# New orders of the steps on TensorE, ScalarE and VectorE in a two-block, two-layer kernel

## What is computed

```python
# block 1, for each of 2 layers
h = _rms(x, norm_g[l]); proj = h @ w_in[l]                     # 17 parts
y_a = _gla(gq, gk, gv, ga, ...) * silu(gz)                     # branch a: gated linear attention
y_b = _dsa(bq, bk, bv, iq, ik, iw, ...) * silu(bz)             # branch b: top-k attention
y_c = _diff(cq, ck, cv, ...) * silu(cz)                        # branch c: differential attention
merged = g[:, :, 0]*(y_a @ w_br[l,0]) + g[:, :, 1]*(y_b @ w_br[l,1]) + g[:, :, 2]*(y_c @ w_br[l,2])
x = x + merged @ w_out[l]
# inside _dsa: which keys a query may see
score = einsum('bqhs,bqh->bqs', relu(dots), iwb);  top_val, top_idx = lax.top_k(score, 128)
# inside _gla: the decay of a token
log_a = log_sigmoid(a_lr @ wa2 + ba) / GLA_TAU
# block 2, for each of 2 layers
mod = silu(c) @ w_mod[l] + b_mod[l]                            # six rows of 1024
h = rms_norm(x, norm1) * (1 + scale1) + shift1; proj = h @ w_in
y_pool = pool_mixer(u, ...); y_nsa = nsa_mixer(q, k, v, gates, ...)  # compressed + selected + window
x = x + gate1 * (concat([y_pool, y_nsa]) @ w_out)
h2 = rms_norm(x, norm2) * (1 + scale2) + shift2
x = x + gate2 * (square(relu(h2 @ w_ff1)) @ w_ff2)             # width 4096
```

## Time and profile before

| | us |
|---|---|
| three runs | 2622.38, 2625.09, 2625.36 |
| median | 2625.09 |
| profiled execution: span | 2625.7 |
| PE busy | 2471.4 (94%) |
| DVE busy | 1365.9 (52%) |
| POOL busy | 1280.2 (49%) |
| ACT busy | 954.5 (36%) |
| mean granted TensorE clock | 0.972 of full |

### The profile page before, as it was taken

How to read it: one execution, slowest core, us unless ns; L and a number is a source line. 1 busy time by engine, 2 the same in 40 slices (tenths; PEclk the granted TensorE clock), 3 DMA queues, 4 the chain that set the end, 5 groups by cost and what they waited for, 6 DMA issues and landing times.

```text
span 2625.7 us, 36622 instructions
## 1 busy us (share of the span) xinstructions
PE 2471.4 (94%) x12303; PEld 1982.3 (75%) x12303; DVE 1365.9 (52%) x2835; ACT 954.5 (36%) x1691; POOL 1280.2 (49%) x2900
## 2 busy tenths in 40 slices
PE   7989999999998999999998898999998889899999
PEld 6676878678867687867887657888888656788887
DVE  5596343654459624365366445554467754522325
ACT  4433243432443234343244553322224354332221
POOL 4453736356545273635644104676765301466563
PEclk9999999999999899999999899999999999999999
DMA  4231514135423151413532002454534101233332
GB/s 160 87 97 50 176 49 144 49 105 184 134 65 97 52 173 57 137 49 113 180 97 61 25 1 65 153 167 146 165 120 109 53 17 30 68 97 96 97 96 81
DMA packets 132193, 256.18 MB, mean 98 GB/s; under 512 B 21914, under 2 KB 28588, under 8 KB 132012
## 3 DMA queue, kind: packets, MB, share of 16 engines
q1 hardware_dynamic: 132012, 253.83, 30.9%
HBM read 249.60 MB, written 4.19 MB: 97 GB/s over the span
## 4 chain that ended last, share of the span: by engine, by line
PE 80%; DVE 14%; ACT 3%; issue 2%; POOL 0%; DMA 0%; DVEq 0%; SPq 0%; ACTq 0%
PE ps L826 66%; PE ps L780 4%; DVE arena L1778 2%; DVE top L1776 2%; PE ps L1077 2%; PE ps L973 1%; PE ps L1126 1%; PE ps L888 1%; PE ps L953 1%; DVE maskb L1783 1%; PE ps L948 1%; PE ps L1064 1%; DVE ps L1714 1%; DVE yarena L1966 1%; ACT arena L1439 1%
## 5 line engine op out<-in xcount | busy, mean ns | idle before, releaser
L757 POOL TENSOR_TENSOR wl<-raw,wh 128x128 fp32r<-128x128 f32 (+2 forms) x2896 | 1280.0, 482 | 1318.8 <-ACT wh L1147 1317.6
L826 PE MATMUL ps<-wh,hTh 128*128 128x512 f32 (+3 forms) x1600 | 637.6, 398 | 3.1 <-POOL wl L757 1.9
L826 PE MATMUL ps<-wl,hTh 128*128 128x512 f32 (+3 forms) x1600 | 618.4, 387 | 0.0
L826 PE MATMUL ps<-wh,hTl 128*128 128x512 f32 (+3 forms) x1600 | 618.2, 386 | 0.0
L1147 ACT ACTIVATE wh<-raw 128x1024 fp32r<-128x1024 f32 (+2 forms) x362 | 378.2, 1049 | 523.1 <-PE ps L826 287.5
L826 PEld LDWEIGHTS ps<-wh,hTh 128*128 128x128 f32 x1600 | 306.2, 191 | 77.6 <-issue 16.7
L826 PEld LDWEIGHTS ps<-wh,hTl 128*128 128x128 f32 x1600 | 305.5, 191 | 58.9
L826 PEld LDWEIGHTS ps<-wl,hTh 128*128 128x128 f32 x1600 | 306.2, 191 | 51.1
L826 PE MATMUL ps<-hTh,wh 128*128 128x512 f32 (+2 forms) x704 | 259.0, 368 | 3.9 <-DVE hTl L1718 2.4
L826 PE MATMUL ps<-hTh,wl 128*128 128x512 f32 (+2 forms) x704 | 257.7, 366 | 0.0
L826 PE MATMUL ps<-hTl,wh 128*128 128x512 f32 (+2 forms) x704 | 257.7, 366 | 0.0
(11 more groups left out here) (274 smaller groups left out, 3199.3 us busy)
## 6 DMA issues: line engine op xcount, KB each, us to landing
raw<-in_w_in_dram SPq DMA_DIRECT2D x160, 512.0 KB, 3.6
raw<-in_w_ff_dram SPq DMA_DIRECT2D x128, 512.0 KB, 3.7
modw<-in_w_mod_dram SPq DMA_DIRECT2D x96, 512.0 KB, 4.7
raw<-in_w_br_dram SPq DMA_DIRECT2D x24, 512.0 KB, 3.7
raw<-in_w_out_dram SPq DMA_DIRECT2D x24, 512.0 KB, 3.6
xm<-in_x_dram SPq DMA_DIRECT2D x8, 512.0 KB, 4.1
raw<-in_w_out_dram SPq DMA_DIRECT2D x16, 256.0 KB, 3.7
raw<-in_w_in_dram SPq DMA_DIRECT2D x8, 408.0 KB, 3.2
```

What stands on the lines that cost most here:

```text
L757: last = pool.tensor_tensor(low[part], whole[part], high[part], ALU.subtract)
L826: last = pe.matmul(*args, start=(q == 0 and c == 0 and n_pass == 0), stop=(q == u["quarters"] - 1 and c == u["chunks"] - 1 and n_pass == 2))
```

## The change

Only tables and the code that reads them are changed: no operation is added, taken away or given another size. `FIRST` and `SECOND` list the same steps in another order. `MOVED` has a third table, for PE, and the two for ACT and DVE are longer, several hundred pairs in all. Evacuations and `mod` steps can now be named in it, for one layer or both. PE's moves are applied first, and ACT's and DVE's sequences start from PE's; SP's loads, the weight halves and the scratch slots go by PE's sequence. The norm heads keep their places. Of the diff, cut to a line or two of each table:

```diff
 FIRST = """
-index.2.0 index.2.1 bk.1.0/ index.2.2 index.2.3 bk.1.0 index.2.4 index.2.5 bk.1.1/ index.2.6 index.2.7 bk.1.1
...
+index.2.1 topk.1.0 index.2.2 index.2.3 bk.0.3 bk.1.0/ index.2.4 bk.1.0 index.2.5 bk.1.1/ index.2.6 index.2.7
...
+topk.3.7 topk.3.8 decay1.2 gv.1.3 gz.0.0 topk.3.9 gz.0.1 decay1.3 gz.0.2 gz.0.3 decay3.0 gz.1.0 decay3.1
...
-MOVED = {"act": """prob_turn.b.0.0>logit_exp.b.0.2 pair_exp.2.0.0>pool_band.1 pair_exp.1.1.2>pool_band.1 logit_exp.c.3.3>gate11.1.1
...
+MOVED = {"pe": """evac.bq.1>bq.1.0 q_turn.b.1>bq.1.2 evac.iq.0>iq.1.3 evac.small.0>index.0.4
...
+                  evac.fd60.0>fd61.0.1 evac.fd60.1>evac.fd60.0 evac.fd61.1>evac.fd61.0 fd71.0.1>evac.fd71.0
...
+                  mod.6.0>bz.1.3 mod.5.0>y_tok.a.2 mod.4.0>bz.0.1 mod.3.0>index.0.4 mod.2.0>iq.1.3
...
+                  prob.c.1.3>logit_max.c.2.0 prob.c.2.0>prob.c.1.3 evac.br10.0>logit_max.c.2.1
```

More of the change, by code:

```diff
@@ L106 @@
[L106 to L109, removed]
-bz.0.3 y_turn.a.1 gla_out.3 y_tok.a.3 y_turn.a.2 bz.1.0 bz.1.1/ bz.1.1 bz.1.2 y_turn.a.3 bz.1.3 gate00.0.0
@@ new lines @@
+pair_value.0.0 cmp_logits.1 pair_value.0.1 rstd.eq.1 pair_logits.1.1.0 pair_turn.1.0.0 pair_prob.1.0.0
+pool_band.0 pair_prob.1.0.2 pair_max.1.1.2 pair_prob.1.1.0 cmp_turn2.1 pair_logits.1.1.2 pair_prob.1.1.2
+o_split.0 pair_logits.2.0.0 pair_turn.1.0.2 pair_exp.1.0.0 pair_max.2.0.0 pair_exp.1.0.2 pool_band.1
+pair_exp.1.1.0 cmp_prob.2 cmp_logits.2 pair_value.1.0 pair_prob.2.0.0 pair_prob.2.0.1 pair_max.2.0.1
+pair_max.2.0.2 pair_max.2.0.3 pair_turn.1.1.0 pair_exp.1.1.2 pool.0 pair_logits.2.0.1 pair_turn.1.1.2 cmp_prob.3
@@ new lines @@
+pool.1 pair_logits.2.0.2 pair_turn.2.0.0 pair_exp.2.0.0 pair_value.1.1 cmp_turn2.2 pair_exp.2.0.1
+pair_prob.2.0.2 pair_prob.2.0.3 pair_exp.2.0.2 pair_exp.2.0.3 pair_logits.2.0.3 pair_turn.2.0.1 pair_exp.2.1.0
+pair_logits.2.1.0 pair_turn.2.0.2 pair_max.2.1.0 o_split.1 pool_band.2 pair_turn.2.0.3 pair_max.2.1.1
+pair_exp.2.1.1 pair_logits.2.1.1 pair_exp.2.1.2 pair_turn.2.1.0 pair_logits.2.1.2 pair_prob.2.1.0 pair_max.2.1.2
+pair_prob.2.1.1 cmp_logits.3 cmp_in.1 pair_exp.2.1.3 pair_logits.2.1.3 pair_logits.3.0.0 pair_exp.3.0.0
@@ new lines @@
+pair_turn.2.1.1 pair_prob.2.1.2 pool.2 pair_max.2.1.3 pair_value.2.0 pair_turn.2.1.2 pair_logits.3.0.1
+pair_max.3.0.0 pair_turn.2.1.3 pair_prob.2.1.3 pair_logits.3.0.2 pair_exp.3.0.1 cmp_turn2.3 pool_band.3
+pair_turn.3.0.0 pair_prob.3.0.0 pair_prob.3.0.1 pair_prob.3.0.2 pair_max.3.0.1 pair_prob.3.0.3 pair_value.2.1
+pair_logits.3.0.3 pair_exp.3.0.2 pair_turn.3.0.1 pair_exp.3.0.3 pair_max.3.0.2 pair_logits.3.1.0 pair_exp.3.1.0
+pool.3 pair_turn.3.0.2 pair_logits.3.1.1 pair_turn.3.0.3 pair_logits.3.1.2 pair_prob.3.1.0 pair_exp.3.1.1
@@ L193, in steps @@
             out.append((kind, named[rest[0]], *rest[1:]))
+        elif kind in ("stats", "scale", "turn"):
+            out.append((kind, (rest[0], l), *rest[1:]))
+        elif kind == "mod":
+            out.append((kind, rest[0]))
+        elif kind in ("columns", "constants"):
+            out.append((kind,))
         else:
@@ L335, in orders @@
 def orders(line, units):
-    own = {"pe": line}
-    for engine, moved in MOVED.items():
-        own[engine] = seq = list(line)
+    own = {}
+    for engine in ("pe", "act", "dve"):
+        own[engine] = seq = list(own["pe"] if own else line)
         for l in sorted({u["l"] for u in units}):
             named = {u["name"]: i for i, u in enumerate(units) if u["l"] == l}
-            for pair in moved.split():
+            for pair in MOVED[engine].split():
                 step, place = (steps(word, l, named)[0] for word in pair.split(">"))
-                seq.remove(step)
-                seq.insert(seq.index(place) + 1, step)
+                if step[0] not in ("mod", "columns", "constants") or pair.split(">")[0].endswith(f".{l}"):
+                    seq.remove(step)
+                    seq.insert(seq.index(place) + 1, step)
@@ L395, in build @@
     own = orders(line, units)
+    line = own["pe"]
     start = []
```

325 lines of the change are left out of this document (234 added, 91 removed).

## The result

| | us |
|---|---|
| changed kernel, four runs | 2527.9 to 2533.96, median 2530.03 |
| kernel before, four runs | 2622.22 to 2625.36, median 2623.74 |
| ratio | 0.9638 (0.9622 to 0.9654, 95%) |
| profiled execution, span | 2528.0 (before 2625.7) |

The account below looks back on a forecast made before the run. PE was taken as the bound, busy 2471.4 of 2625.7 us. From 2625: -26 for block 1's waits, -26 for block 2's, -12 for the clock, +9 for new waits, giving 2570 us, range 2540 to 2624.

Parts of the forecast that it names:

- decay1.3: Block 1's decay step: PE's 7.6 us wait for DVE's top-k chain goes, -6.9 a layer, bounds -3.3 and -7.6.
- The GLA wait: Block 1's GLA output: the first wait, 3.6 us, grows by about 1.5; all its waits together +0.6.
- The transposes behind L1457: Block 2's second and third tiles: waits of 2.8 and 2.5 us for ACT's copy shrink by 2.4 and 1.9.
- prob_turn.c.1.3: Block 1's differential attention: a 3.7 us wait behind DVE's evacuation of br10.0 falls to about 1.4, -2.3.
- I count half: Block 1's shorter waits, 1.3 us and less, sum to about 7; half taken as gain, -3.7.
- I take 3 back: Block 2's listed gains of -15.9 a layer, cut by 3 for new waits between coupled steps, to -12.9.
- a fifth to a quarter: Clock term: share regained of 51 us lost to lowered clock in three attention stages, -12, bounds 0 and -30.
- +9: New waits elsewhere: a microsecond or so in nine rearranged places, bounds 0 and +25.
- index and key: Block 1's index and key waits: 1.6 us, of which -0.8 goes, bounds 0 and -1.6.
- rival A: Whole kernel: all waits go as listed, 58 us, and 20 of clock: 2547 us, chance 0.17.
- Rival D: Whole kernel slower: mod products stall ahead of evacuations while POOL runs, up to 2660 us, chance 0.13.
- The mask that I had expected to meet POOL idle: Block 1's top-k: the 7.79 us mask, moved earlier, meets POOL idle and the chain ends 7.3 us sooner.

Follow-up runs that it names:

- decay_alone: Kernel before, with PE's decay1.3 alone moved behind two sweep steps, DVE's top-k as before: 2630.52 us, ratio 1.0016.
- br10_alone: Kernel before, with only DVE's evacuation of br10.0 moved behind a later probability step: 2620.82 us, ratio 0.9988.
- decay_shift: Kernel before, with decay1.3, the decay3 steps and the four state steps of PE moved to their changed places: 2613.71 us, ratio 0.9965.
- block1_new: New orders on all three engines up to block 1's last sweeps, the old orders behind: 2586.79 us, ratio 0.9883 to the kernel before.
- attn2_new: New orders in the two attention stages of block 2 alone, old orders elsewhere: 2546.64 us, ratio 0.9741 to the kernel before.
- filler: Kernel before, with 52 transposes that nobody reads put on PE ahead of decay1.3: 2617.47 us, ratio 0.9972.
- undo_pair: Changed kernel, with PE's pair_turn.1.0.2 put back directly behind cmp_turn2.1 in both layers: 2532.99 us, ratio 0.9635 to the kernel before.

## Why the forecast was wrong

**What held.** PE bounds the kernel, and waits and clock are all that an order can give: 72.6 of 154.3 us of idle and 25.1 of busy time went, nothing else. `decay1.3` was forecast at -6.9 a layer and gave -7.6 and -7.4. That it came so near is partly luck: the release was forecast at 192.3 and came at 194.1, PE was forecast at 192.5 and came at 195.6, and the two errors, 1.8 and 3.1 us, go the same way and nearly cancel. The GLA wait was forecast to stay and stayed (3.7, forecast 4 to 5 and growing; it was 3.6). The transposes behind L1457: forecast -2.4 and -1.9, and 2.8 and 1.8 went. `prob_turn.c.1.3`: forecast -2.3, measured -3.7. Of my signs, PE's idle was to be about 110 and is 81.7, and one sign of a wrong forecast came: a new wait of over 2 us in the feed-forward (3.24).

**The step that failed** is the one by which I took the sum apart: "I count half", "I take 3 back", "a fifth to a quarter", and "+9" for new waits. Each is a discount on what the rows listed, and none has a row. What the runs showed in their place:

| term | forecast | measured |
|---|---|---|
| waits of block 1, both layers | -26 | -38 |
| waits of block 2's attention | -26 | -38 |
| clock | -12 | -25 |
| new waits, feed-forward included | +9 | +5 |

The measured rows are from the two tables of stages above: length less PE's busy time for the waits, the change of the whole busy time for the clock, and the idle of the feed-forward for the last; new waits inside a stage with new orders are in its net. In block 1 the short waits were the largest miss: of the differential attention's stage, 6.7 us with the 3.7 of `prob_turn.c.1.3`, 5.4 and 6.6 us went, and all 2.3 of index and key. In block 2 no wait over 0.8 is left in the attention behind the norm head, where there had been seven of over 1.3. That is rival A, which I gave 0.17 and 2547, and which itself stopped at 20 us of clock and 58 of waits.

**Why the discount was tempting and wrong.** I feared that a wait taken away comes back at the next place. It does: `decay_alone` and `br10_alone` gained nothing, the wait moved on to a step behind it. But this is so of a single move. `decay_shift` moved all that hangs on one chain at once and won 4 of 7.6 us by that on PE's side alone (DVE's top-k, which the change also starts earlier, untouched), and `block1_new` with `attn2_new` show no loss between the stages. That the many other waits went for the same reason is argued from this one case and not shown wait by wait. The test that I should have made is in the orders and in the trace: for each step behind the freed one, whether it too has work put ahead of it. For the decay step I had looked at `decay1.3` only; the change also moves `decay3` and the state steps, and without that, by `decay_alone`, PE's part of my -6.9 would have been near 0.

**What the decay wait was.** I priced 7.6 us as the length of top-k, and the stall of the mask as something beside it. The unheld masks of `attn2_new` and `filler` show that the stall is nearly all of the wait. The new order of top-k puts the mask where DVE has gaps behind it, so that the wait goes and stays away; against a layer in which the mask isn't held, this term is 0.3 us.

**The clock.** I held that a fifth to a quarter of 51 us would come back; 25 did, and 24 of this net are from the attention of block 2 (block 1 gave 5, the feed-forward took 4). Its stages held 42 of the 51 by my own figures. `attn2_new` won 29 us of busy time in them. Behind the decay wait the clock was 0.60 over six microseconds before and 1.00 in `attn2_new`, which had no such wait. But in `undo_pair` one wait of 2.0 among few others cost nothing that can be seen at the clock. That it takes many waits close together, as between the second and the fourth token tile of block 2 before, is what the traces suggest and no run isolates. There the same steps in the same order took 68.7 us in layer 0 and 60.4 in layer 1 of the kernel before (clock 0.78 and 0.92), 64.2 and 67.3 in `filler` (and as much in `br10_alone`, which has no filler), 61.7 and 60.5 in `decay_shift`. The kernel before, then the changed one:

```profile
1461.60:1530.30 68.70, 58.41 (x318) 38.02 (x318) 31.36 (x67) 30.83 (x80) 0.00 (x0) 0.78 0.00 1
2111.40:2171.80 60.40, 49.50 (x318) 31.53 (x317) 31.26 (x67) 30.83 (x80) 0.00 (x0) 0.92 0.00 1
```

```profile
1406.80:1452.40 45.60, 44.08 (x312) 28.28 (x310) 32.07 (x70) 33.75 (x81) 11.82 (x26) 0.96 0.00 1
2028.70:2075.80 47.10, 45.57 (x312) 28.98 (x310) 32.00 (x70) 33.74 (x81) 11.77 (x26) 0.93 0.00 1
```

The stretch that answers to it in the changed kernel takes 45.6 and 47.1 (312 matmuls where it was 318). So part of the loss comes and goes in one and the same order. Which of the waits bring the clock down stays open: the waits of that stretch weren't filled, since all eight banks are in use there.

**Rival D** had its mechanism seen (a `mod` step and POOL's run ahead of an evacuation, 3.24 us at `fu1.1.0` and 1.7 for the slow step behind it, 4.56 us where it is 2.88), once where it needed seven. It cost 5 us of the 8 that the stage became longer. The product ended at 1580.67, 1.08 us behind the end of POOL's run of 13.94 us (1579.59), so it got to work only when that run was over. The page "SBUF — State Buffer" of the Trainium skill, section "SBUF: two separate sides", has the lock held "for the whole instruction", by which the product would wait for one subtraction; this trace too disagrees, since POOL's run is 32 of them. The mask that I had expected to meet POOL idle took 3.13 us instead of 7.79, also within a run: the stall was shortened and not gone, and the term didn't need it, since 6.47 us of idle stand behind it.

## What to carry to other kernels

When many steps are moved together, price each wait by asking whether everything that hangs on the same chain has work put in front of it; if so count all of the wait, and if not, count little of it, since it moves on. A flat discount for coupling fits neither case. Look along the chain for an instruction far over its median, as the mask of 7.79 us beside 0.66: a wait that hangs on it comes and goes by itself, and a time can be compared only when the trace says which case it was. Where the trace shows a stage with a lowered clock and dense short waits, give the clock a term of its own and let its bound reach the loss of that stage; here 24 of 42 us came back.

## What the runs showed of the hardware that I had not expected

One and the same mask, at the same place in DVE's order and 5.8 us into a run of GpSimd subtractions, was held for 7.8 us in 10 of 12 cases and took 0.66 in the other two; what decides it isn't known. In `attn2_new` the layer with the short one was 13 us shorter than in the kernel before. The kernel before spread over 2606 to 2639 us from run to run with its mean clock between 0.979 and 0.967, while the changed kernel and those near it, on the same chips, stayed within 2515 to 2540 and between 0.987 and 0.994. Fewer waits may make the time steadier, and so may a mask whose stall no longer reaches PE; no run tells the two apart, and the kernel before was run more often (64 times beside 4 to 6 each).
